# A decoder layer on one core: the feed-forwards' 22 tiles grouped 4, 10, 8 in place of 6, 8, 8

## The chip, the cores and the metric

The kernel runs on one core of a Trainium2 chip. The time is in device microseconds, from the start to the end of the program on that core; lower is better. TensorE (PE) multiplies matrices, VectorE (DVE) and ScalarE (ACT) work elementwise, GpSimd (POOL) does small side work, and SyncE (SP) issues most of the DMAs.

## What is computed

One layer for 512 prompt tokens and 32 sample tokens, D_MODEL = 1024: a half-step feed-forward, a mixing block of two attention kinds, a second half-step feed-forward, and a gated embedding. The change concerns the two feed-forwards, which the reference computes as follows.

```
D_FF = 2816

def swiglu(h, w_in, w_out):
    gu = h @ w_in
    g, u = jnp.split(gu, 2, axis=-1)
    return (jax.nn.silu(g) * u) @ w_out

x = x + 0.5 * rmsnorm(swiglu(rmsnorm(x, f1_pre), f1_in, f1_out), f1_post)
...
x = x + 0.5 * rmsnorm(swiglu(rmsnorm(x, f2_pre), f2_in, f2_out), f2_post)
```

## The kernel before

All activations stay on chip, features on partitions and the T = 544 tokens in two halves of 272. Each fp32 product is made from three fp32r matmuls: an operand is split into a high part (a copy by ACT, `w_hi`, `a_hi`, `h_hi`) and a low part (what remains, a subtraction by DVE, `w_lo`, `a_lo`, `h_lo`), and TensorE adds high x high, low x high and high x low (helper `dense`, L584).

**Feed-forward.** D_FF is 22 tiles of 128 rows. They are worked in three groups, `GROUPS`. For each group, an up stage makes the group's h tiles (silu(gate) x up), and a down stage multiplies them by the group's columns of the output weight and adds 8 output tiles into `y`. The h tiles of one group lie in `h_hi` and `h_lo`, which hold `G_MAX` tiles each.

- The first group (`f1_up0`, `f2_up0`) is made by plain products: per tile 8 blocks of input features x gate and up x 3 x 2 halves = 96 matmuls.
- The later groups (`up1`, `up2`) are made by `up_mixed` (L796), a scheme of seven products of blocks instead of eight. It splits tokens, input features and gate/up in two each. One tile is 7 products of 4 feature blocks x 3 matmuls = 84 matmuls. For it DVE adds blocks of weights (`mix_front`, L2015 to L2020), and needs seven activation blocks.
- These activation blocks are built while the first group runs: `block_values` (L2070), `block_difference` and `block_sum` (L2084 to L2097) on DVE, then for each of seven `block_high` on ACT (L1465) and `block_low` on DVE (L2077). Blocks 3 to 6 overwrite the plain input `a_hi`, `a_lo`; so blocks 3 to 5 wait for `a_gone`, which TensorE raises while it works on the group's last plain tile.
- A down stage has 8 products of (group size) x 6 matmuls. Its product reads the h tiles in order and waits for each one's low part (`h_tiles`).

**Queues.** Every engine has its instructions in a fixed order, written by hand. On DVE a tile of the first group is: two multiplies that take the sums out of PSUM (`out_of`, L1995, L1996), the product with silu (`product_of`, L2102), `h_lo` (L2001), and the split of the next weights (L1880). ACT has silu (L1423), `h_hi` (L1428) and the weights' high part (L1303). In the first down stage ACT also takes every product out of PSUM (L1510). `plain_end` is the end of the first group: around the last plain tile it holds block copies, the last tile's chain, and the split of the second down weight.

**Weights.** Two raw slots and two split slots are used in turn. SP's load of weight tile w waits until tile w - 2 is split; ACT's copy of a weight waits until the product before last has ended (`psum_full`).

In other places of the program, buffers of later use lie over those of earlier ones: `proj` (the projections of the mixing block) shares its memory, `hold_h`, with the h tiles, and the weights of the output projection are placed into free parts of it:

```
GROUPS = (6, 8, 8)
PLAIN = GROUPS[0]
hold_h = sb("hold_h", [P, 24 * T])
PLACED[W0["out"] + 2] = (h_flat[0][:, 4 * T:4 * T + SLOT], h_flat[1][:, 0:SLOT])
```

Of the kernel before, what the change touches and what calls it, by code (L numbers as in the profile page):

```python
# [18 lines left out]
ACT = mybir.ActivationFunctionType  # L19

P = 128
D_MODEL = 1024
SEQ = 512
DEC_BATCH = 8
# [14 lines left out]
GROUPS = (6, 8, 8)  # L39
G_FIRST = (0, 6, 14)  # L40
# [77 lines left out]
def build(nc, a, o):  # L118
# [13 lines left out]
    with ctx:  # L132
# [34 lines left out]
        kl_new = sb("kl_new", [N_SAMPLE, P])  # L167
# [7 lines left out]
        glr = sb("glr", [GLA_RANK, 2, HALF])  # L175
# [25 lines left out]
        hold_h = sb("hold_h", [P, 24 * T])  # L201
# [12 lines left out]

        work_flat = work[:].rearrange("p a t -> p (a t)")
# [153 lines left out]
        for name in (f"f1_down{ENDS}", f"f2_down{ENDS}"):  # L369
            for n in range(4):  # L370
                PLACED[W0[name] + 4 + n] = tuple(t_[:, G_MAX * P * n:G_MAX * P * (n + 1)] for t_ in a_flat)
# [923 lines left out]
        def _(act):  # L1295
# [171 lines left out]
            def plain_end(name):  # L1467


                f, up0, down0, st = int(name == "f2"), f"{name}_up0", f"{name}_down0", Step(PLAIN - 1)  # L1470
                split(st, up0, ticket(st, up0)[0])
                for n in range(3, 6):
                    act.wait_ge(sig["a_gone"], 3 * f + n - 2)
                    block_high(f, n)
                split(Step(0), down0, ticket(Step(0), down0)[0])
                up_gate(up0, st)
                up_high(up0, st)
                block_high(f, 6)
                act.wait_ge(sig["t_lo"], 7 * f + 4)
                down_first(Step(0), *ticket(Step(0), down0))  # L1480
# [92 lines left out]
            up("f1_up0")(Step(3), *ticket(Step(3), "f1_up0"))  # L1573
            stage("f1_up0", PLAIN, up("f1_up0"), first=4, end=PLAIN - 1)
# [30 lines left out]
            def keys_out(p):  # L1605
                act.wait_ge(sig["klt_full"], p + 1)
                if p:

                    act.wait_ge(sig["u_full"], p)
                    act.wait_ge(sig["klb_ready"], p)  # L1610
                fn(kl_nat, PS[:, 7, :].rearrange("p (c n) -> p c n", c=N_CH), ACT.Copy)
                fn(kl_new[:], PS[0:N_SAMPLE, 6, 64:64 + P], ACT.Copy).then_inc(sig["klt_out"], 1)
# [172 lines left out]
            split_edge("out", 1, T0["merge"])  # L1785
            split_edge("out", 2, T0["merge"])
# [24 lines left out]
            split_edge("f2_up0", 4, T0["f2_up0"] + 2)  # L1811
# [3 lines left out]
            up("f2_up0")(Step(3), *ticket(Step(3), "f2_up0"))  # L1815
            stage("f2_up0", PLAIN, up("f2_up0"), first=4, end=PLAIN - 1)
# [55 lines left out]
        def _(dve):  # L1872
# [231 lines left out]
            def plain_end(name, j):  # L2104
# [4 lines left out]
                split(st, up0)  # L2109
# [112 lines left out]
            up("f1_up0", 0)(Step(3), *ticket(Step(3), "f1_up0"))  # L2222
            stage("f1_up0", PLAIN, up("f1_up0", 0), first=4, end=PLAIN - 1)
# [24 lines left out]
            v.tensor_tensor(glr[:], PS[0:GLA_RANK, 4 * quad:4 * quad + 2, 0:HALF], rstd[0:GLA_RANK, 0],  # L2248
# [101 lines left out]
            def new_keys(p):  # L2350

                dve.wait_ge(sig["klt_out"], p + 1)
                if p:
                    dve.wait_ge(sig["sn_full"], 4 * p)
                v.tensor_tensor(kl_batch, kl_new[:].unsqueeze(1).broadcast_to([N_SAMPLE, DEC_BATCH, P]),
                                batch_mask[0:N_SAMPLE, :].unsqueeze(2).broadcast_to([N_SAMPLE, DEC_BATCH, P]),
                                ALU.mult).then_inc(sig["klb_ready"], 1)
# [260 lines left out]
            split_edge("f2_up0", 4)  # L2618
# [11 lines left out]
            up("f2_up0", 4)(Step(3), *ticket(Step(3), "f2_up0"))  # L2630
            stage("f2_up0", PLAIN, up("f2_up0", 4), first=4, end=PLAIN - 1)
# [313 lines left out]
```

## Time and profile before

| | |
|---|---|
| Median of 3 runs | 1181.22 us (1180.56 to 1181.26) |
| Span of the profiled execution | 1178.6 us |
| TensorE busy | 1159.9 us, 98%, 9234 matmuls |
| VectorE busy | 778.8 us, 66% |
| ScalarE busy | 548.2 us, 47% |
| First feed-forward, from the first matmul | 7.3 to about 374 us |
| Second feed-forward | about 739 to 1092 us |

A matmul's start-to-start distance is shorter than its duration, since they are pipelined: the mean of one is 290 ns, but 432 of them fill 54.31 us. "Idle before" in brackets is the time that an engine stood before an instruction, and what it then waited for. The chain of work that ended last tells which engine sets the end.

### The profile page before, as it was taken

How to read it: one execution, taken by the hardware profiler on the slowest of the kernel's cores; microseconds unless marked ns; L12 is line 12 of the kernel's file. 1: busy time of each engine (PE TensorE's matmuls, PEld its weight loads, DVE VectorE, ACT ScalarE, POOL GpSimd, SP SyncE). 2: the span in 40 equal slices, each digit the busy share in tenths (PEclk: the TensorE clock that was granted, in tenths of full speed). 3: DMA queues.
4: the chain of work that ended last, by engine and by line, in shares of the span. 5: the costliest groups of instructions: out<-in, count | busy, mean ns of one | idle time of the engine just before them, and what ended most of it. 6: DMA issues, size and time to landing. Idle time of an engine off the chain costs nothing.

```text
span 1178.6 us, 23067 instructions
## 1 busy us (share of the span) xinstructions
PE 1159.9 (98%) x9234; PEld 1120.3 (95%) x9234; DVE 778.8 (66%) x1076; ACT 548.2 (47%) x759; POOL 105.6 (9%) x138
## 2 busy tenths in 40 slices
PE   7999999999999999999999999999999999999997
PEld 7999999999999999999877699999999999999996
DVE  6853887368844965655379737863788458864766
ACT  5433555235543532312368745533555225543655
POOL 1600000000002012122050010000000000002102
PEclk9999999999999999999999999999999999999999
DMA  6213331232224032213047151113421233215202
GB/s 220 86 30 132 112 107 54 90 131 91 81 72 152 12 108 73 72 57 113 1 152 241 58 179 37 42 56 100 140 85 64 90 125 107 89 54 178 74 1 76
DMA packets 45404, 110.27 MB, mean 94 GB/s; under 512 B 5458, under 2 KB 11618, under 8 KB 45202
## 3 DMA queue, kind: packets, MB, share of 16 engines
q1 hardware_dynamic: 43522, 103.13, 26.2%
q0 software_dynamic: 1232, 5.01, 1.2%
q8 instruction: 54, 0.88, 0.3%
q10 hardware_dynamic: 576, 1.08, 0.2%
q14 instruction: 20, 0.16, 0.1%
HBM read 103.57 MB, written 5.64 MB: 93 GB/s over the span
## 4 chain that ended last, share of the span: by engine, by line
PE 91%; DVE 5%; ACT 3%; issue 1%; DMA 1%; ACTq 0%; DVEq 0%
PE PS L584 42%; PE PS L796 29%; PE PS L597 11%; PE PS L916 1%; PE PS L766 1%; PE PS L620 1%; PE PS L943 1%; DMA raw<-in_f_in 1%; PE PS L976 1%; ACT w_hi L1303 0%; PE PS L979 0%; DVE w_extra L2453 0%; PE PS L1020 0%; DVE extra L2440 0%; DVE w_lo L1880 0%
## 5 line engine op out<-in xcount | busy, mean ns | idle before, releaser
L1303 ACT ACTIVATE w_hi<-raw 128x1024 fp32r<-128x1024 f32 (+2 forms) x77 | 93.2, 1210 | 154.4 <-PE PS L584 129.6
L1880 DVE TENSOR_TENSOR w_lo<-raw,w_hi 128x1024 fp32r<-128x1024 f32 (+2 forms) x76 | 107.9, 1420 | 83.1 <-ACT w_hi L1303 82.7
L796 PE MATMUL PS<-a_lo,w_hi 128*128 128x272 f32 x512 | 148.7, 290 | 0.0
L796 PE MATMUL PS<-a_hi,w_lo 128*128 128x272 f32 x512 | 147.6, 288 | 0.0
L584 PE MATMUL PS<-a_hi,w_hi 128*128 128x272 f32 x656 | 139.5, 294 | 8.1 <-DVE w_lo L2181 7.3
L796 PE MATMUL PS<-a_hi,w_hi 128*128 128x272 f32 x512 | 147.4, 288 | 0.0
L584 PE MATMUL PS<-a_lo,w_hi 128*128 128x272 f32 x656 | 136.4, 289 | 0.0
L584 PE MATMUL PS<-a_hi,w_lo 128*128 128x272 f32 x656 | 136.0, 289 | 0.0
L584 PE MATMUL PS<-h_hi,w_hi 128*128 128x272 f32 x576 | 119.5, 289 | 0.2
L584 PE MATMUL PS<-h_hi,w_lo 128*128 128x272 f32 x576 | 119.2, 288 | 0.0
L584 PE MATMUL PS<-h_lo,w_hi 128*128 128x272 f32 x576 | 118.8, 288 | 0.0
L584 PEld LDWEIGHTS PS<-a_hi,w_hi 128*128 128x128 f32 x656 | 103.2, 189 | 12.3 <-issue 10.4
L584 PEld LDWEIGHTS PS<-a_lo,w_hi 128*128 128x128 f32 x656 | 103.8, 190 | 0.0
L584 PEld LDWEIGHTS PS<-a_hi,w_lo 128*128 128x128 f32 x656 | 103.5, 190 | 0.0
L796 PE MATMUL PS<-b_tail,w_hi 128*128 128x272 f32 x512 | 98.0, 289 | 0.0
L796 PEld LDWEIGHTS PS<-a_hi,w_hi 128*128 128x128 f32 x512 | 96.6, 189 | 0.0
L796 PEld LDWEIGHTS PS<-a_hi,w_lo 128*128 128x128 f32 x512 | 96.4, 188 | 0.0
L796 PEld LDWEIGHTS PS<-a_lo,w_hi 128*128 128x128 f32 x512 | 96.1, 188 | 0.0
L584 PEld LDWEIGHTS PS<-h_hi,w_hi 128*128 128x128 f32 x576 | 90.5, 188 | 0.8 <-DVE h_lo L2001 0.6
L584 PEld LDWEIGHTS PS<-h_lo,w_hi 128*128 128x128 f32 x576 | 90.5, 189 | 0.0
L584 PEld LDWEIGHTS PS<-h_hi,w_lo 128*128 128x128 f32 x576 | 89.9, 189 | 0.0
L796 PEld LDWEIGHTS PS<-b_tail,w_hi 128*128 128x128 f32 x512 | 80.3, 188 | 0.0
(473 smaller groups left out, 2618.9 us busy)
## 6 DMA issues: line engine op xcount, KB each, us to landing
raw<-in_f_in SPq DMA_DIRECT2D x86, 512.0 KB, 4.0
raw<-in_f_out SPq DMA_DIRECT2D x64, 256.0 KB, 2.8
raw<-in_w_rest SPq DMA_DIRECT2D x40, 256.0 KB, 2.8
raw<-in_f_out SPq DMA_DIRECT2D x32, 192.0 KB, 2.4
raw<-in_w_out SPq DMA_DIRECT2D x8, 512.0 KB, 4.6
raw<-in_ple_w_gate SPq DMA_DIRECT2D x8, 512.0 KB, 4.2
x<-in_x SPq DMA_DIRECT2D x8, 272.0 KB, 7.1
raw<-in_w_in SPq DMA_DIRECT2D x4, 512.0 KB, 4.1
```

The lines of the kernel that those rows point to most:

```text
L584: last = mm(PS[0:width, 4 * quad + 2 * c + half, 0:HALF], wt[:, cols], act[:, k, half * HALF:(half + 1) * HALF], start=(k == 0 and n == 0) ...
L597: last = mm(PS[0:width, 4 * quad + 2 * c + half, 0:HALF], wt[:, cols], act[:, k, tok], start=(k == 0 and n == 0), stop=(k == n_k - 1 and n ...
L620: last = mm(PS[:, 4 * quad + 2 + half, 0:HALF], ones[:], squares[:, tok], start=(k < summed), stop=(k == KD - 1))
L766: last = mm(PS[:, 4 * (t % 2) + 2 * c + half, 0:HALF], wt[:, slot, col:col + P], act[:, k, half * HALF:(half + 1) * HALF], start=(k == 0 a ...
L796: last = mm(PS[:, 4 * quad + bank, 0:HALF], w_[:, k * P:(k + 1) * P], a_[:, k, :], start=(start and k == 0 and i == 0), stop=(stop and k = ...
L916: last = mm(PS[:, 2 + hh, tok], k_[r, tok], q_[r, tok], start=True, stop=True)
L943: last = mm(PS[:, 7, n * 256:n * 256 + 256], kl_batch[:, 2 * part + n, :], gv_new[:, p * 256:(p + 1) * 256], start=True, stop=True)
L976: last = mm(PS[:, 2 + hh, tok], gv_nat[:, c, h * P:(h + 1) * P], att[p][:, N_CH * hh + c, :], start=True, stop=(c == 0))
L1303: fn(pair[0][:, 0:width], raw[:, slot, 0:width], ACT.Copy).then_inc(sig["split_hi"], 1)
L1880: v.tensor_tensor(pair[1][:, 0:width], raw[:, slot, 0:width], pair[0][:, 0:width].bitcast(F32), ALU.subtract).then_inc(sig["split_lo"], 1)
```

## The change

`GROUPS` becomes (4, 10, 8): the first group of each feed-forward has 4 plain tiles, the second 10 mixed tiles, the third 8 as before. So two tiles of each feed-forward pass from `dense` to `up_mixed`.

`h_hi` and `h_lo` grow to 10 tiles each. Memory for that comes from three places: `kl_new` gets a place in a buffer that holds `glr`, the GpSimd DMAs' descriptor scratch is halved to 8192 bytes, and `hold_h` is 28 instead of 24 rows of T. As the h buffers reach further into the projections, the third weight tile of the output projection now lies over keys of the mixing block, and ACT waits for the store of these keys (`k_stored`) before it writes there.

The steps of tiles 3 to 5 in the first group go: tile 3 is now the one that `plain_end` handles, and the split after tile 2 is already that of the first down weight.

```
-GROUPS = (6, 8, 8)
-G_FIRST = (0, 6, 14)
+GROUPS = (4, 10, 8)
+G_FIRST = (0, 4, 14)
...
-        kl_new = sb("kl_new", [N_SAMPLE, P])
...
-        glr = sb("glr", [GLA_RANK, 2, HALF])
+        glr_all = sb("glr_all", [P, 2, HALF])
+        glr = glr_all[0:GLA_RANK]
...
-        hold_h = sb("hold_h", [P, 24 * T])
+        hold_h = sb("hold_h", [P, 28 * T])
...
+        kl_new = scratch(glr_all[:].rearrange("p a t -> p (a t)"), 0, [N_SAMPLE, P])
...
-                split(st, up0, ticket(st, up0)[0])
...
-            up("f1_up0")(Step(3), *ticket(Step(3), "f1_up0"))
-            stage("f1_up0", PLAIN, up("f1_up0"), first=4, end=PLAIN - 1)
             plain_end("f1")
...
+            act.wait_ge(sig["k_stored"], 16)
             split_edge("out", 2, T0["merge"])
...
-            split_edge("f2_up0", 4, T0["f2_up0"] + 2)
+            split(Step(3), "f2_up0", ticket(Step(3), "f2_up0")[0])
...
-            up("f2_up0")(Step(3), *ticket(Step(3), "f2_up0"))
-            stage("f2_up0", PLAIN, up("f2_up0"), first=4, end=PLAIN - 1)
             plain_end("f2")
...
-                split(st, up0)
                 block_low(f, 3)
                 block_low(f, 4)
                 out_of(up0, j, st, t, quad, use)
...
-            up("f1_up0", 0)(Step(3), *ticket(Step(3), "f1_up0"))
-            stage("f1_up0", PLAIN, up("f1_up0", 0), first=4, end=PLAIN - 1)
             block_low(0, 2)
             plain_end("f1", 0)
...
-    nc = bacc.Bacc("TRN2", target_bir_lowering=False, num_devices=1)
+    nc = bacc.Bacc("TRN2", target_bir_lowering=False, num_devices=1, dynamic_dma_scratch_size=8192)
```

VectorE's queue of the kernel before, first feed-forward, from the low part of h tile 2 (L2001) to the last plain tile's chain. L1995 and L1996 take a tile out of PSUM, L2077 is `block_low`; the line numbers of the two kernels differ by three.

```order
L2001 TENSOR_TENSOR h_lo<-work,h_hi 128x544
L1880 TENSOR_TENSOR w_lo<-raw,w_hi 128x2048
L2097 SCALAR_TENSOR_TENSOR y<-extra,y 128x4x272
L1995 TENSOR_TENSOR work<-PS,rstd 128x544
L1996 TENSOR_TENSOR work<-PS,rstd 128x544
L2102 TENSOR_TENSOR work<-work 128x544
L2001 TENSOR_TENSOR h_lo<-work,h_hi 128x544
L1880 TENSOR_TENSOR w_lo<-raw,w_hi 128x2048
L1995 TENSOR_TENSOR work<-PS,rstd 128x544
L1996 TENSOR_TENSOR work<-PS,rstd 128x544
L2102 TENSOR_TENSOR work<-work 128x544
L2001 TENSOR_TENSOR h_lo<-work,h_hi 128x544
```

The same queue of the changed kernel, from the same instruction:

```order
L1998 TENSOR_TENSOR h_lo<-work,h_hi 128x544
L1877 TENSOR_TENSOR w_lo<-raw,w_hi 128x512
L2094 SCALAR_TENSOR_TENSOR y<-extra,y 128x4x272
L2074 TENSOR_TENSOR b_tail<-y,b_tail 128x1088
L2074 TENSOR_TENSOR a_lo<-y,a_hi 128x1088
L2074 TENSOR_TENSOR a_lo<-extra,a_hi 128x1088
L1992 TENSOR_TENSOR work<-PS,rstd 128x544
L1993 TENSOR_TENSOR work<-PS,rstd 128x544
L2099 TENSOR_TENSOR work<-work 128x544
L1877 TENSOR_TENSOR w_lo<-raw,w_hi 128x512
L1998 TENSOR_TENSOR h_lo<-work,h_hi 128x544
```

Between the sum L2097 (now L2094) and the next take-out stood nothing; now three `block_low` stand there, and that take-out belongs to the last plain tile.

ScalarE's queue at the same place, before. L1423 is silu, L1428 `h_hi`, L1465 `block_high`:

```order
L1428 ACTIVATE h_hi<-work 128x544
L1465 ACTIVATE b_tail<-y 128x1088
L1423 ACTIVATE work<-work 128x544
L1428 ACTIVATE h_hi<-work 128x544
L1303 ACTIVATE w_hi<-raw 128x2048
L1423 ACTIVATE work<-work 128x544
L1428 ACTIVATE h_hi<-work 128x544
L1303 ACTIVATE w_hi<-raw 128x768
L1465 ACTIVATE a_hi<-y 128x1088
L1465 ACTIVATE a_hi<-extra 128x1088
L1465 ACTIVATE a_hi<-hold_h 128x1088
L1303 ACTIVATE w_hi<-raw 128x768
```

and in the changed kernel, where these are L1424, L1429 and L1466:

```order
L1429 ACTIVATE h_hi<-work 128x544
L1466 ACTIVATE b_tail<-y 128x1088
L1466 ACTIVATE a_hi<-y 128x1088
L1466 ACTIVATE a_hi<-extra 128x1088
L1466 ACTIVATE a_hi<-hold_h 128x1088
L1304 ACTIVATE w_hi<-raw 128x512
L1424 ACTIVATE work<-work 128x544
L1429 ACTIVATE h_hi<-work 128x544
```

The four `block_high` stand in one row, behind `h_hi` of tile 2 and ahead of the second down weight's copy.

## Rows read from the trace of the kernel before

**Rows 1.** The page: busy time of engines; the chain that ended last.

```profile
PE 1159.9 (98%) x9234; PEld 1120.3 (95%) x9234; DVE 778.8 (66%) x1076; ACT 548.2 (47%) x759; POOL 105.6 (9%) x138
...
PE 91%; DVE 5%; ACT 3%; issue 1%; DMA 1%; ACTq 0%; DVEq 0%
```

**Rows 2.** The chain by time, two pieces: start us, us, what.

```profile
29.44 54.31 PE PS L584 x432
...
120.18 84.75 PE PS L796 x672
```

**Rows 3.** TensorE at down0's start: start us, us, instruction, idle before.

```profile
83.58 0.42 PE L584 MATMUL PS<-h_hi,w_hi 128*128 128x272 f32 x2
...
87.59 0.30 PEld L584 LDWEIGHTS PS<-h_hi,w_hi 128*128 128x128 f32 x2 [0.31 <-DVE h_lo L2001]
...
799.14 0.30 PEld L584 LDWEIGHTS PS<-h_hi,w_hi 128*128 128x128 f32 x2 [0.31 <-DVE h_lo L2001]
```

**Rows 4.** Timeline, ACT and DVE at down0's end; then load medians.

```profile
106.79 0.63 ACT L1510 ACTIVATE y<-PS 128x544 f32 x1 [3.16 <-PE PS L584]
...
108.18 0.96 DVE L1880 TENSOR_TENSOR w_lo<-raw,w_hi 128x768 fp32r<-128x768 f32 x1 [3.56 <-ACT w_hi L1303]
...
113.98 0.69 DVE L2015 TENSOR_TENSOR hold_w<-raw 128x512 f32<-128x512 f32 x1 [0.34 <-DMA raw<-in_f_in]
...
115.91 0.69 DVE L2020 TENSOR_TENSOR sq<-hold_w,raw 128x512 f32<-128x512 f32 x1
...
117.84 1.76 DVE L2023 TENSOR_TENSOR w_lo<-raw,w_hi 128x1536 fp32r<-128x1536 f32 x1 [1.24 <-ACT w_hi L1436]
...
819.73 0.96 DVE L1880 TENSOR_TENSOR w_lo<-raw,w_hi 128x768 fp32r<-128x768 f32 x1 [3.54 <-ACT w_hi L1303]
...
825.98 0.69 DVE L2015 TENSOR_TENSOR hold_w<-raw 128x512 f32<-128x512 f32 x1 [0.78 <-DMA raw<-in_f_in]
...
raw<-in_f_in SPq DMA_DIRECT2D x86, 512.0 KB, 4.0
```

**Rows 5.** Timeline of DVE and ACT, plain tiles of the first feed-forward.

```profile
53.96 2.28 DVE L1880 TENSOR_TENSOR w_lo<-raw,w_hi 128x2048 fp32r<-128x2048 f32 x1
...
56.16 1.28 DVE L2097 SCALAR_TENSOR_TENSOR y<-extra,y 128x1088 f32<-128x1088 f32 x1
...
57.48 1.12 ACT L1465 ACTIVATE b_tail<-y 128x1088 fp32r<-128x1088 f32 x1 [4.58 <-DVE y L2097]
...
59.67 0.73 DVE L1995 TENSOR_TENSOR work<-PS,rstd 128x544 f32<-128x544 f32 x1 [2.23 <-PE PS L584]
...
75.34 1.28 DVE L2077 TENSOR_TENSOR b_tail<-y,b_tail 128x1088 fp32r<-128x1088 f32 x1
...
83.78 0.72 DVE L1995 TENSOR_TENSOR work<-PS,rstd 128x544 f32<-128x544 f32 x1 [3.59 <-PE PS L584]
...
86.81 0.72 DVE L2001 TENSOR_TENSOR h_lo<-work,h_hi 128x544 fp32r<-128x544 f32 x1
```

**Rows 6.** Timeline of DVE and ACT, plain tiles of the second feed-forward.

```profile
762.01 2.29 DVE L1880 TENSOR_TENSOR w_lo<-raw,w_hi 128x2048 fp32r<-128x2048 f32 x1
...
772.37 1.29 DVE L2097 SCALAR_TENSOR_TENSOR y<-extra,y 128x1088 f32<-128x1088 f32 x1
...
773.69 1.11 ACT L1465 ACTIVATE b_tail<-y 128x1088 fp32r<-128x1088 f32 x1 [5.60 <-DVE y L2097]
```

**Rows 7.** TensorE's first matmuls; windows at the end: busy, PEclk.

```profile
7.30 0.79 PE L584 MATMUL PS<-a_hi,w_hi 128*128 128x272 f32 x2 [7.30 <-DVE w_lo L2181]
...
11.34 0.41 PE L584 MATMUL PS<-a_hi,w_hi 128*128 128x272 f32 x2
...
1172.00:1174.00 2.00, 0.17 (x1) 0.00 (x0) 1.96 (x5) 0.54 (x2) 0.00 (x0) 1.00 0.94 328
...
1175.00:1176.00 1.00, 0.00 (x0) 0.00 (x0) 0.00 (x0) 0.00 (x0) 0.00 (x0) 0.52 1.05 359
```

**Rows 8.** Timeline of GpSimd: the store of the keys.

```profile
555.46 0.55 POOL L2833 DMA_DIRECT2D out<-proj  x1
```

More of the change, by code:

```diff
@@ L370, in build @@
             for n in range(4):
-                PLACED[W0[name] + 4 + n] = tuple(t_[:, G_MAX * P * n:G_MAX * P * (n + 1)] for t_ in a_flat)
+                PLACED[W0[name] + 4 + n] = tuple(t_[:, GROUPS[ENDS] * P * n:GROUPS[ENDS] * P * (n + 1)] for t_ in a_flat)
         tail_flat = b_tail[:].rearrange("p a b k t -> p (a b k t)")
@@ L1611, in keys_out @@
                 fn(kl_nat, PS[:, 7, :].rearrange("p (c n) -> p c n", c=N_CH), ACT.Copy)
-                fn(kl_new[:], PS[0:N_SAMPLE, 6, 64:64 + P], ACT.Copy).then_inc(sig["klt_out"], 1)
+                fn(kl_new, PS[0:N_SAMPLE, 6, 64:64 + P], ACT.Copy).then_inc(sig["klt_out"], 1)
             act.wait_ge(sig["small_in"], 32)
@@ L2247, in _ @@
             full(dve, t)
-            v.tensor_tensor(glr[:], PS[0:GLA_RANK, 4 * quad:4 * quad + 2, 0:HALF], rstd[0:GLA_RANK, 0],
+            v.tensor_tensor(glr, PS[0:GLA_RANK, 4 * quad:4 * quad + 2, 0:HALF], rstd[0:GLA_RANK, 0],
                             ALU.mult).then_inc(psum_free[quad], 1)
@@ L2354, in new_keys @@
                     dve.wait_ge(sig["sn_full"], 4 * p)
-                v.tensor_tensor(kl_batch, kl_new[:].unsqueeze(1).broadcast_to([N_SAMPLE, DEC_BATCH, P]),
+                v.tensor_tensor(kl_batch, kl_new.unsqueeze(1).broadcast_to([N_SAMPLE, DEC_BATCH, P]),
                                 batch_mask[0:N_SAMPLE, :].unsqueeze(2).broadcast_to([N_SAMPLE, DEC_BATCH, P]),
@@ L2617, in _ @@
             block_difference(1, 0)
-            split_edge("f2_up0", 4)
+            split(Step(3), "f2_up0")
             st = Step(2)
@@ L2629, in _ @@
             block_sum(1, 1)
-            up("f2_up0", 4)(Step(3), *ticket(Step(3), "f2_up0"))
-            stage("f2_up0", PLAIN, up("f2_up0", 4), first=4, end=PLAIN - 1)
             block_low(1, 2)
```

## Prediction

> **What bounds the kernel now.** Read the chain of work that ended last: TensorE holds 91% of it [rows 1]. The long pieces of that chain show how densely: 432 plain matmuls in 54.31 us without a break, and 672 matmuls of a mixed group in 84.75 us [rows 2]. So TensorE's number of matmuls sets the time of a feed-forward, as long as VectorE (DVE) and ScalarE (ACT) have the next operands ready. The places where they are only just ready matter more here than averages. There are two in each feed-forward. The first is the step from the plain tiles to the first down projection (down0): in both feed-forwards TensorE's weight load waits 0.31 us for the last h tile's low part [rows 3]. The second is the step from down0 to the first mixed group [rows 4]. Nothing waits there now, but I shall show how little room is left.
>
> **What the change takes away.** A plain tile is 96 matmuls, at 54.31 / 432 = 0.1257 us each 12.07 us. A mixed tile is 7 products of 4 x 3, so 84 matmuls, at 84.75 / 672 = 0.1261 us each 10.59 us [rows 2]. Two tiles of each feed-forward pass from plain to mixed: 4 x (12.07 - 10.59) = 5.9 us less. The down projections keep their matmuls (22 h tiles x 8 x 6 in all), only cut 4 + 10 + 8 instead of 6 + 8 + 8. So down0's product is 24 matmuls (3.02 us) instead of 36 (4.52 us), down1's is 60 instead of 48. The longer down1 has more cover than before, and its wider weight split (1280 columns) falls into 7.5 us of product; the mixed group of 10 is the same loop run more often. Both at nothing.
>
> **First cost: the step from plain tiles to down0.** Down0's product reads its h tiles in order and can run until it needs the last one. That is 5 tiles of 6 matmuls, 3.77 us of cover, before; now 3 tiles, 2.26 us. Before, the last tile's chain on DVE began at 83.78, ended with the low part at 86.81 + 0.72, and TensorE went on at 87.59 [rows 3, 5]: 3.81 us. The narrower weight split in this chain (512 columns for 768) takes some 0.06 us off, since the h tile's own ACT copy is next late: 3.75 us. With that alone the wait would grow by 1.4 us.
>
> But the order on DVE moves too. The copies of the blocks for the mixed products (L2077, 1.28 us each; DVE starts its next instruction 0.08 us before the end, as at 53.96 and 56.16, so one every 1.20 us [rows 5]) were spread over two more tiles. Now three of them stand between the sum L2097 and the last tile's chain. In the first feed-forward: the split before the sum takes 0.69 instead of 2.28 us (the 512-wide DVE row at 113.98 [rows 4]), so the sum starts at 56.16 - 1.59 = 54.57 and ends at 55.85. ACT's copy of that block follows its end by 0.04 and takes 1.12, to 57.01 [rows 5]. Then DVE copies three low parts, 57.04 + 3 x 1.20 = 60.64 (ACT's copies take 1.12 us and stay ahead), and only then takes up the last tile, 1.0 us later than the 59.67 at which tile 3 was taken up before [rows 5]. TensorE gets the last low part at 60.64 + 3.75 = 64.39. It begins down0 two plain tiles earlier, 83.58 - 24.14 = 59.44, and runs dry at 61.70 [rows 3]. **Wait 2.7 us in place of 0.25** (87.59 less 83.58 + 30 x 0.1257): cost 2.5 us.
>
> In the second feed-forward DVE is later by itself, as the blocks are made while the first tiles run. The split at 762.01 shrinks from 2.29 to 0.69, everything after moves up by 1.6 us, and the sum at 772.37 starts at 770.77, ends 772.06 [rows 6]. ACT's copy to 773.21, three low parts to 776.84, chain to 780.59. Down0 began at 799.14 - 0.25 - 3.77 = 795.12 before [rows 3], begins at 770.98 now and runs dry at 773.24. **Wait 7.35 us in place of 0.25**: cost 7.1 us. Bounds for both together: if the copies cost no queueing, 1.4 each (2.8); if a copy waits for ACT's one in each case, up to 1 us more each (11.6). I take 9.6, since the order of the queues is fixed and every duration has a row.
>
> **Second cost: the step from down0 to the mixed group.** Its weights are 1 MB. The load starts when down0's seventh weight tile is split, and that waits on the product two places back. Before: ACT takes out product 4 at 106.79, the split ends at 108.18 + 0.96 = 109.14, the first sum of the new weights starts at 113.98, four sums and the low part follow (113.98, 115.91, 117.84 + 1.76 = 119.60) [rows 4], and TensorE needs them at about 120.0. The low part waited for ACT's copy there; without that it starts 2.55 us after the first sum. After: both splits are narrower by about 0.2 and 0.27 us, so from taking out product 4 (call it 0) the split ends at 1.86, the load lands at 1.86 + 4.84 = 6.70, the low part ends at 6.70 + 2.55 + 1.76 = 11.01, TensorE starts at 11.06. It ran out at three products later, 3 x 3.02 - 0.28 = 8.78. **Wait 2.3 us**, where there was none. In the second feed-forward the load took 825.98 - 820.69 = 5.29 us (the split at 819.73 takes 0.96) [rows 4], so 2.75 us. Together 5.0. Bounds: 1.8 us more each if the next 1 MB load, which now starts 3.0 instead of 4.5 us after this one, shares its bandwidth; 1 us less each if the load lands as early as the 4.0 us median of its halves [rows 4]. I take 5.0, from the two pairs of rows.
>
> A page of the Trainium skill prices the load otherwise: "DMA: Bandwidth & Descriptors", section "Anatomy of one DMA", gives about 2.0 us plus the bytes at 436 GB/s for one GpSimd-issued transfer, an estimate of 4.4 us for 1 MB; the rows of this case say 4.84 and 5.29. By the page the waits would be 1.3 us shorter together.
>
> Down0's inner steps stay covered: the split ends 1.86 us after a product is taken out, the running product 3.02 - 0.28 = 2.74 after it, so 0.9 us are left on each of the six. If that room were gone, each tenth of a microsecond would cost 0.6 us in a feed-forward.
>
> **Third cost: TensorE's clock.** At the start TensorE stood for 7.3 us, and its first matmuls come 0.22 to 0.23 us apart, half speed, until 11.34 [rows 7]: 18 matmuls took 4.04 instead of 2.26 us, 1.8 us lost. At the end its last matmul is over by 1172.2, and from 1175 on the granted clock is 0.52, the 1.2 GHz level [rows 7]. So a rest of 2.8 us was followed by the lower level there. The new rest of 7.4 us lies far beyond, so I add 1.8 us once. The three shorter ones (2.7, 2.3, 2.75 us) lie just at or under that 2.8; I take nothing for them and keep 5.4 us as the bound.
>
> The Trainium skill, "TensorE: Matmul & The Clock Gate", section "HAM oscillation", says that waits between bursts of matmuls put the clock back down, so that each burst starts slow. [...]
>
> **At nothing:** ACT's new wait for the stored keys stands ahead of the out-projection splits near 665 us; the store is issued at 555.46 [rows 8], a hundred microseconds earlier. The halved scratch serves GpSimd's few DMAs, none of which anyone waits for. If it delayed one, 1 us on the key store would still be hidden. The two moved small buffers change no instruction.
>
> **The sum.** -5.9 + 2.5 + 7.1 + 2.3 + 2.75 + 1.8 = +10.5 us. The profiled execution spans 1178.6 us and the median is 1181.22, 2.6 us outside the span, which the change doesn't touch. Forecast 1191.8 us.
>
> **Rivals.**
> 1. The clock holds through the 7.4 us rest: 1190.0. For it, no rest within the run before shows a fall, all being short; against it, both ends of the run. 0.12.
> 2. The clock falls in shorter waits too: one of them 1193.6, all three 1197.2. The tail shows the fall after 2.8 us; against it, TensorE was thinly used before that tail and densely before these. 0.18.
> 3. Half the stalls: the load lands early and DVE's copies fit better, some 4 us less, 1185 to 1188. 0.08.
> 4. The other side: the saved matmuls stand and the cover suffices. This is one mechanism, the last plain tile's chain on DVE and the load behind it both finishing inside down0's shorter products; then -5.9, 1175.3. It decides where the four waits sum to under 5.9 us, 40% of what I get. For it: ACT and DVE are 47% and 66% busy only [rows 1], and down0's inner steps keep room. Against: the waits follow from queue order and one load, not from averages. 0.06 faster, and 0.03 that it comes out even.
>
> The likeliest case has 0.53. The range reaches over rivals 1, one extra clock fall, and most of 3: 1186.5 to 1196.5. A measurement of this kernel can tell about 0.2%, 2.4 us, from no change: faster by more 0.06, within 0.03, slower 0.91.
>
> **What the profile after would show.** TensorE's count falls by 48 to 9186. At about 62 us and 773 us TensorE waits for the h tile's low part, 2.7 and 7.4 us; at about 85 and 806 it waits for the mixed weights' low part, 2.3 and 2.8 us. Matmuls after the 7 us rest stand 0.23 us apart for some 18. If the waits at 62 and 773 are equal, my reading of DVE's order is wrong; if there are none before the mixed group, the load was issued or landed earlier than I hold.

## The result: 1.1% slower

| | before | after |
|---|---|---|
| Median | 1181.24 us (4 runs) | 1194.14 us (4 runs, 1191.35 to 1195.09) |
| Ratio to before | | 1.0108, 95% interval 1.0096 to 1.0121 |
| Span of the profiled execution | 1178.6 us | 1192.5 us |
| TensorE's matmuls | 9234 | 9186 |

The forecast was 1191.8 us, slower. The median lies 2.3 us above it, inside the range.

The page of the changed kernel, to be read against [rows 1]: busy time, the granted clock in the 40 slices, and the shares of the chain that ended last.

```profile
PE 1159.1 (97%) x9186; PEld 1119.1 (94%) x9186; DVE 795.1 (67%) x1100; ACT 560.6 (47%) x779; POOL 105.7 (9%) x138
...
PEclk9999999999999999999999999989999999999999
...
PE 84%; DVE 9%; ACT 3%; issue 2%; DMA 2%; SPq 0%; DVEq 0%; ACTq 0%
```

48 matmuls are gone, yet TensorE's busy time fell by 0.8 us only, mostly since some of the others ran at half speed (the 8 in the clock's row is the longest such stretch). In the chain TensorE's share went from 91% to 84% and DVE's from 5% to 9%: there are now stretches in which TensorE does not set the end. The list of TensorE's waits (what waited for, sum, times, longest) names them:

```profile
PE PS L585 <- DVE h_lo L1998: 9.6, 2, 7.1
PE PS L585 <- DVE w_lo L2177: 7.0, 1, 7.0
PE PS L797 <- DVE w_lo L2020: 5.7, 2, 2.9
```

The middle one is the start of the program and was there before. The other two are the two steps of the prediction, each once per feed-forward. The first step in the first feed-forward, VectorE and TensorE (start us, us, instruction, idle before):

```profile
57.02 1.29 DVE L2074 TENSOR_TENSOR b_tail<-y,b_tail 128x1088 fp32r<-128x1088 f32 x1 [1.18 <-ACT b_tail L1466]
...
60.63 0.72 DVE L1992 TENSOR_TENSOR work<-PS,rstd 128x544 f32<-128x544 f32 x1
...
63.59 0.72 DVE L1998 TENSOR_TENSOR h_lo<-work,h_hi 128x544 fp32r<-128x544 f32 x1
...
61.47 0.41 PE L585 MATMUL PS<-h_hi,w_lo 128*128 128x272 f32 x2
64.37 0.52 PE L585 MATMUL PS<-h_hi,w_hi 128*128 128x272 f32 x2 [2.50 <-DVE h_lo L1998]
```

Three block copies run from 57.02 to 60.63, only then is the last tile taken out, and TensorE, dry since 61.72 (61.47 and two matmuls), goes on at 64.37: 2.65 us. In the second feed-forward the same rows stand later against TensorE, because the sum L2094 is later:

```profile
774.73 1.29 DVE L2094 SCALAR_TENSOR_TENSOR y<-extra,y 128x1088 f32<-128x1088 f32 x1
...
780.81 0.72 DVE L1992 TENSOR_TENSOR work<-PS,rstd 128x544 f32<-128x544 f32 x1
...
777.00 0.41 PE L585 MATMUL PS<-h_hi,w_lo 128*128 128x272 f32 x2
784.55 0.82 PE L585 MATMUL PS<-h_hi,w_hi 128*128 128x272 f32 x2 [7.15 <-DVE h_lo L1998]
```

Dry from 777.25 to 784.55, 7.3 us. The second step, down0 to the mixed group, answers to [rows 4]: the last split before the load (L1877), the first use of the loaded weights (L2012), their low part (L2020), and TensorE at both of its ends.

```profile
78.80 0.69 DVE L1877 TENSOR_TENSOR w_lo<-raw,w_hi 128x512 fp32r<-128x512 f32 x1 [2.38 <-ACT w_hi L1304]
...
84.93 0.69 DVE L2012 TENSOR_TENSOR hold_w<-raw 128x512 f32<-128x512 f32 x1 [2.49 <-DMA raw<-in_f_in]
...
87.47 1.75 DVE L2020 TENSOR_TENSOR w_lo<-raw,w_hi 128x1536 fp32r<-128x1536 f32 x1
...
86.03 0.41 PE L585 MATMUL PS<-h_hi,w_lo 128*128 128x272 f32 x2
89.27 0.52 PE L797 MATMUL PS<-b_extra,w_hi 128*128 128x272 f32 x2 [2.84 <-DVE w_lo L2020]
...
812.07 0.52 PE L797 MATMUL PS<-b_extra,w_hi 128*128 128x272 f32 x2 [2.90 <-DVE w_lo L2020]
```

The split ends at 79.49, the weights are used from 84.93: 5.44 us (5.57 in the second feed-forward, from 802.15 to 807.72). TensorE stands for 3.0 us here, and for 3.06 there.

Last the clock, in windows: busy time with counts for each engine, granted clock, DMA share, GB/s.

```profile
90.00:93.00 3.00, 3.00 (x18) 3.00 (x17) 2.97 (x5) 0.40 (x1) 0.00 (x0) 0.59 0.81 268
...
785.00:790.00 5.00, 5.00 (x24) 5.00 (x24) 2.59 (x3) 1.14 (x2) 0.00 (x0) 0.50 0.24 72
812.00:815.00 3.00, 2.93 (x23) 2.93 (x24) 2.97 (x5) 0.62 (x2) 0.00 (x0) 1.00 0.55 137
```

After the 7.3 us rest TensorE ran at its 1.2 GHz level until 790.16: 24 matmuls in 5.61 us instead of 3.02, so 2.6 us lost. After the 3.0 us wait of the first feed-forward the clock fell too, but late: the matmuls are 0.125 us apart from 89.27 to 90.51 and 0.22 apart behind it. The mixed group there took 107.71 us for its 840 matmuls, the same group in the second feed-forward, behind a wait of 3.06 us, took 106.20 at full clock: 1.5 us.

The account of the span: -5.9 (matmuls) + 2.4 (2.65 for 0.25) + 7.05 (7.3 for 0.25) + 3.0 + 3.06 + 2.6 + 1.5 = 13.7 us. Measured: 1192.5 - 1178.6 = 13.9. The medians are 12.9 apart, since the profiled execution of the changed kernel (1194.62 us) was 0.5 us above its median, and 2.1 us of it lay outside the span where I had counted 2.6.

### The profile page after: what moved, and what is told of

Same layout as the page of the kernel before. It is cut to its first block, busy times and chain, and to the rows that moved or that the text cites. A ratio compares the mean times of both kernels' runs of the same rounds, so it can differ in the third digit from the quotient of the medians.

```text
span 1192.5 us, 23120 instructions
## 1 busy us (share of the span) xinstructions
PE 1159.1 (97%) x9186; PEld 1119.1 (94%) x9186; DVE 795.1 (67%) x1100; ACT 560.6 (47%) x779; POOL 105.7 (9%) x138
## 4 chain that ended last, share of the span: by engine, by line
PE 84%; DVE 9%; ACT 3%; issue 2%; DMA 2%; SPq 0%; DVEq 0%; ACTq 0%
PE PS L585 33%; PE PS L797 32%; PE PS L598 10%; DMA raw<-in_f_in 2%; PE PS L917 1%; PE PS L767 1%; PE PS L621 1%; PE PS L944 1%; DVE w_lo L1877 1%; PE PS L977 0%; DVE work L2099 0%; DVE hold_h L2067 0%; ACT w_hi L1304 0%; PE PS L980 0%; DVE h_lo L1998 0%
## 5 line engine op out<-in xcount | busy, mean ns | idle before, releaser
L797 PE MATMUL PS<-a_lo,w_hi 128*128 128x272 f32 x576 | 166.5, 289 | 0.0
L797 PE MATMUL PS<-a_hi,w_lo 128*128 128x272 f32 x576 | 166.4, 289 | 0.0
L1304 ACT ACTIVATE w_hi<-raw 128x1024 fp32r<-128x1024 f32 (+3 forms) x73 | 85.6, 1172 | 168.0 <-PE PS L585 138.9
L1877 DVE TENSOR_TENSOR w_lo<-raw,w_hi 128x1024 fp32r<-128x1024 f32 (+3 forms) x72 | 98.8, 1373 | 73.2 <-ACT w_hi L1304 73.2
L797 PE MATMUL PS<-b_tail,w_hi 128*128 128x272 f32 x576 | 111.4, 291 | 0.0
L585 PE MATMUL PS<-a_lo,w_hi 128*128 128x272 f32 x528 | 110.0, 290 | 0.0
L585 PE MATMUL PS<-a_hi,w_lo 128*128 128x272 f32 x528 | 109.8, 289 | 0.0
L797 PEld LDWEIGHTS PS<-a_hi,w_hi 128*128 128x128 f32 x576 | 108.5, 188 | 0.0
L797 PEld LDWEIGHTS PS<-a_hi,w_lo 128*128 128x128 f32 x576 | 108.4, 188 | 0.0
L797 PEld LDWEIGHTS PS<-a_lo,w_hi 128*128 128x128 f32 x576 | 108.3, 188 | 0.0
L585 PEld LDWEIGHTS PS<-h_hi,w_hi 128*128 128x128 f32 x576 | 91.6, 190 | 10.3 <-DVE h_lo L1998 10.1
L585 PEld LDWEIGHTS PS<-a_hi,w_hi 128*128 128x128 f32 x528 | 83.4, 190 | 11.8 <-issue 10.2
L797 PEld LDWEIGHTS PS<-b_tail,w_hi 128*128 128x128 f32 x576 | 91.5, 190 | 0.0
L1437 ACT ACTIVATE w_hi<-raw 128x1536 fp32r<-128x1536 f32 x36 | 53.7, 1491 | 69.4 <-PE PS L797 55.4
L585 PEld LDWEIGHTS PS<-a_lo,w_hi 128*128 128x128 f32 x528 | 83.9, 191 | 0.0
```

Of the source, the lines that this page charges most:

```text
L585: last = mm(PS[0:width, 4 * quad + 2 * c + half, 0:HALF], wt[:, cols], act[:, k, half * HALF:(half + 1) * HALF], start=(k == 0 and n == 0) ...
L797: last = mm(PS[:, 4 * quad + bank, 0:HALF], w_[:, k * P:(k + 1) * P], a_[:, k, :], start=(start and k == 0 and i == 0), stop=(stop and k = ...
L1304: fn(pair[0][:, 0:width], raw[:, slot, 0:width], ACT.Copy).then_inc(sig["split_hi"], 1)
L1437: fn(w_cols(name[:2], 0, 3)[0], raw[:, slot, 0:3 * BLOCK], ACT.Copy).then_inc(sig["split_hi"], 1)
L1877: v.tensor_tensor(pair[1][:, 0:width], raw[:, slot, 0:width], pair[0][:, 0:width].bitcast(F32), ALU.subtract).then_inc(sig["split_lo"], 1)
```

## The experiments

Every kernel was run beside the kernel before on the same chip. On the first chip that had medians of 1180.67 and 1180.79 us (21 runs each), on the second of 1180.53 us (13 runs).

**1. The memory part alone**, groups 6, 8, 8 as before.

```
 GROUPS = (6, 8, 8)
...
-        hold_h = sb("hold_h", [P, 24 * T])
+        hold_h = sb("hold_h", [P, 28 * T])
...
+            act.wait_ge(sig["k_stored"], 16)
...
+ ..., dynamic_dma_scratch_size=8192)
```

> The kernel before, groups 6, 8, 8, with the change's memory part alone: the DMAs' scratch halved, kl_new in the glr buffer, hold_h of 28 rows, ScalarE's wait for the key store. Theory (the time comes from waits of TensorE that the new grouping makes): within 0.5 us of before, 1181.2. Rival (the halved scratch or the new wait costs something): 1183 or more, with the wait seen near 665 us.

1180.68 us, ratio 0.9999 (0.9990 to 1.0008). The halved scratch, the moved buffers and the wait for the keys cost nothing that can be measured; all 12.9 us are the grouping's.

**2. The last tile's chain ahead of the block copies.** The changed kernel; DVE and ACT take up the last plain tile first and make blocks 2 to 6 behind it, while down0 runs.

```
-                block_low(f, 3)
-                block_low(f, 4)
                 out_of(up0, j, st, t, quad, use)
                 product_of(up0, st, quad, use)
                 split(Step(0), f"{name}_down0")
                 up_low(up0, st)
-                block_low(f, 5)
-                block_low(f, 6)
+                block_low(f, 2)
+                block_low(f, 3)
+                split(Step(1), f"{name}_down0")
+                for c in range(2, 5):
+                    split(Step(c), f"{name}_down0")
+                    block_low(f, c + 2)
...
```

ScalarE's queue is turned in the same way.

> The changed kernel with one order turned: on ScalarE and VectorE the last plain tile's chain stands ahead of the block copies, which follow during down0. Theory (the queue order makes 1.0 us of the first and 4.9 us of the second wait): TensorE's wait at down0 falls from 2.65 to about 1.7 us and from 7.3 to about 2.4 us, and the slow clock after the long one goes (2.5 us): about 8 us less than the changed kernel, 1185 to 1187. Rival (VectorE has simply too much work in that stretch, the order doesn't matter): the copies are then late for a later step, a new wait comes up, and the time stays at 1192 to 1195.

1186.99 us (1185.15 to 1188.57), ratio 1.0059. The waits for the last h tile fell from 9.6 to 3.8 us, and the other step's stayed:

```profile
PE PS L797 <- DVE w_lo L2025: 5.4, 2, 3.0
PE PS L585 <- DVE h_lo L2003: 3.8, 2, 2.3
```

The medians are 7.2 us apart, at the edge of what I expected. The profiled execution was the fastest of the five (1185.15 us), and its span is 9.5 us shorter than the changed kernel's: 5.8 us of that is the first step's waiting, 0.3 the second's, 0.8 the start of the program, which differs between executions of one kernel too (down0 began 0.8 us sooner here), and 2.6 the clock. That fell once (behind the 3.0 us wait that had ended at 801.07; low from 802.4 to 805.8 us, 1.5 us lost) where it had cost 4.1. Its mean is 0.998 there for 0.993, and 0.995 to 0.996 in the other four. So the place of the block copies in the two queues is shown to be the cause of most of the first step's wait. Of what stays, 1.5 us in each is the chain against the shorter cover; the other 0.8 us in the second feed-forward is the block sum (L2094, L2099 in this kernel), which still stands ahead of the take-out: VectorE takes the tile out at 772.29, while ScalarE could begin its copy at 771.54.

**3. The first mixed tile's weights early.** The changed kernel; their 1 MB goes into h tiles that are still free, before the load of down0's fifth weight tile.

```
+        mix_raw = hold_h[:, 4 * T:4 * T + SLOT]
...
+                    if n == 0:
+                        for c in range(4):
+                            load(w0 + c, ...)
+                        for c in range(2):
+                            sp.dma_start(mix_raw[:, c * 1024:(c + 1) * 1024], src[:, c * 1024:(c + 1) * 1024]) ...
```

> The changed kernel with the first mixed tile's 1 MB weight loaded early, into h tiles that are free in the first group, in place of behind down0's seventh weight. Theory (the wait of 3.0 us before each mixed group is the load's landing): the sums on VectorE start at once, TensorE's wait falls to about 1.3 us in each feed-forward, and no clock fall follows it: 3.3 us less, 5 where the clock fell: 1188.5 to 1190.5. Rival (VectorE's and ScalarE's own steps set that wait): unchanged, 1192 to 1195.

1190.35 us (1189.08 to 1191.65), ratio 1.0083: 3.8 us less than the changed kernel.

```profile
PE PS L611 <- DVE h_lo L2024: 9.6, 2, 7.1
...
PE PS L823 <- DVE w_lo L2046: 2.0, 2, 1.0
```

The other step is untouched and this one is down to 1.0 us each. So what was late there was the load; the 1.0 us left is ACT's and DVE's high and low part of 1536 columns. The clock fell behind the first feed-forward's wait of about 2.6 us (low from 64.9 to 68.4 us), and behind the long rest it was low from 778.3 to 785.2 us, so that only 12 matmuls behind the restart at 782.26 were slow and 1.4 us were lost.

**4. Both edits.**

> Both of the two edits above on the changed kernel. Theory: the gains add: waits of about 1.7, 2.4, 1.3 and 1.3 us, no clock fall, 1193.7 - 5.9 - 2.5 - 3.3 - about 1 = 1181 to 1183, level with before. Rival (the two waits hide one another or the mixed tiles cost more than their 84 matmuls): 1185 or more.

1181.52 us (1180.39 to 1183.05, 11 runs), ratio 1.0004 (0.9995 to 1.0013). The waits are those that each edit had left (3.8 and 1.8 us). The two edits together give back 12.6 us, alone 7.2 and 3.8; the 1.6 us beyond that sum are within the scatter of the changed kernel. The clock fell once even here, behind the wait of 2.3 us in the second feed-forward (low from 775.4 to 778.8 us), which cost 1.5 us. Counted from where TensorE ran dry, as in the account of the span above, the four waits are 6.2 us. So the account is -5.9 (matmuls) + 6.2 - 0.5 (the two waits that were there before) + 1.5 (clock) - 0.8 (down0 began at 58.68 us; the kernel before's 83.58 less two plain tiles is 59.44) = +0.5 us, and the span is 0.7 us longer than before.

**5. A rest in the kernel before.** To price a rest apart from the regrouping, DVE makes the low part of block 4 five or nine more times in the second feed-forward, one behind the other and ahead of the last plain tile.

```
+                if f:
+                    for i in range(5):
+                        v.tensor_tensor(B_PAIR[4][1], B_RAW[4], B_PAIR[4][0].bitcast(F32), ALU.subtract) ...
```

> The kernel BEFORE, with nothing changed but a delay: on VectorE in feed-forward 2, ahead of the last plain tile's chain, the low copy of block 4 is made five more times (about 1.3 us each, 6.5 in all, of which 3.8 lies under down0's five covered h tiles), so that TensorE rests about 2.5 to 3 us at the plain to down0 step once. If a rest of this length costs its own length only: 1183.3 to 1183.9. If the granted clock falls behind it as it did once in the changed kernel behind a wait of 3.0 us: 1.8 to 2.5 us more, 1185.2 to 1186.2. My theory says that it can do either, so I expect a scatter between the two over the rounds, with a median of 1184 to 1185.

> The kernel BEFORE with the same delay made longer (nine more copies): TensorE rests about 7.5 to 8 us at feed-forward 2's plain to down0 step, once. My theory (a rest this long always lowers the granted clock for some 25 matmuls behind it, which costs 2.5 to 2.8 us): 1190.7 to 1191.7, and the records show the granted clock at its lower level behind the rest. Rival, a rest costs its own length only: 1188.2 to 1188.9.

1185.35 us (1184.25 to 1187.10) and 1191.10 us (1190.31 to 1191.45). The profile of the first shows TensorE's rest and the clock behind it:

```profile
801.89 0.82 PE L584 MATMUL PS<-h_hi,w_hi 128*128 128x272 f32 x2 [3.04 <-DVE h_lo L2001]
...
802.00:804.00 2.00, 2.00 (x9) 2.00 (x10) 2.00 (x2) 0.32 (x2) 0.00 (x0) 0.50 0.61 197
```

The second:

```profile
807.41 0.82 PE L584 MATMUL PS<-h_hi,w_hi 128*128 128x272 f32 x2 [8.35 <-DVE h_lo L2001]
...
809.00:811.00 2.00, 2.00 (x11) 2.00 (x11) 1.15 (x2) 1.35 (x2) 0.00 (x0) 0.50 0.15 57
```

A rest of 3.04 us made the median 4.6 us longer: 12 matmuls at half speed (801.89 to 804.78) lost 1.4 us beside it. One of 8.35 us made it 10.3 us longer: 18 matmuls (807.41 to 811.66) lost 2.0. Counted from where TensorE ran dry, the rests are 3.2 and 8.5 us. Less the 0.25 that was there before and with the clock that makes 4.35 and 10.25 us, so little is missing. The first median missed the 1184 to 1185 us that I expected: it lies where I had put a fall of the clock, not half-way to no fall. The second is in the expected range, but not by the expected terms: the rest came out 0.4 to 0.9 us longer than I put, and the clock's loss as much smaller. The rival without a loss of clock (1188.2 to 1188.9) falls.

**6. More cover.** As 4, and TensorE takes h tiles 0 to 2 for down0's first two products before it needs h tile 3. DVE also splits the first down weight ahead of the product with silu, not behind it.

```
+                for c in range(2):
+                    ...
+                    for k in range(PLAIN - 1):
+                        ...
+                            dense_half(quad, placed(down0, st), 1, k, PLAIN, H, half)
+                h_tiles(first)(PLAIN - 1)
+                for quad, pair in both:
+                    for half in range(2):
+                        last = dense_half(quad, pair, 1, PLAIN - 1, PLAIN, H, half)
```

> The kernel with both edits (the last plain tile's chain ahead of the block copies; the first mixed tile's weight loaded early: 1181.52 us, TensorE still waits 3.8 us in two waits for h_lo and 1.8 in two for w_lo), and now TensorE takes h tiles 0 to 2 of down0's first TWO products before it needs h tile 3, so that its cover is 6 h-tile pieces (4.5 us) and not 3 (2.26 us). My theory (the waits at plain to down0 are a chain of fixed length against a cover counted in products, and nothing else waits at that place): the wait of feed-forward 1 (1.5) goes to about 0, that of feed-forward 2 (2.3) to about 0.1, so the h_lo waits fall from 3.8 to under 0.5 us and the time to 1178.0 to 1178.8. Rival: the second down weight, now needed 2.3 us sooner, takes the wait over (its split stands behind the same copies): the waits keep their sum or nearly, and the time stays at 1181 to 1182. Rival 2: half of it, with 0.7 to 1.2 us left at feed-forward 2: 1179 to 1180.

1180.64 us (11 runs), 0.9 us less than 4 where I expected about 3. The waits for h tile 3 are gone as expected, and the first rival's wait for a down weight's low part is 0.5 us, once. But another wait, at the third product, took their place, 1.5 us in each feed-forward, so that the first feed-forward gained nothing. Its rows in the first, TensorE, DVE and ACT:

```profile
65.04 0.29 PE L624 MATMUL PS<-h_hi,w_lo 128*128 128x272 f32 x1
66.83 0.51 PE L611 MATMUL PS<-h_hi,w_hi 128*128 128x272 f32 x2 [1.50 <-ACT y L1560]
...
64.81 1.28 DVE L2122 TENSOR_TENSOR a_lo<-y,a_hi 128x1088 fp32r<-128x1088 f32 x1
...
66.12 1.14 ACT L1560 ACTIVATE y<-PS 128x544 f32<-128x544 f32 x2 [0.87 <-DVE a_lo L2122]
```

ACT writes down0's first result over `y`, from which DVE still reads blocks 2 and 3. The copies that experiment 2 moved out of the way are late here: until ACT has emptied the first buffer in PSUM, TensorE cannot begin the third product. Neither of my rivals had named this one.

**7. The first 512 columns apart.** As 6, and the first mixed tile's high and low parts are made in two pieces, so that TensorE can begin with the first.

```
+                if cut:
+                    v.tensor_tensor(lo[:, 0:cut], mix_source(name, st, slot)[:, 0:cut], hi[:, 0:cut].bitcast(F32), ...)
...
+                    if early(name, st):
+                        pe.wait_ge(sig["first_lo"], 3 + (f == "f2"))
```

> As the run before (two products of down0 together), and the first mixed tile's high and low parts of the weight are made with their first 512 columns apart, so that TensorE can begin the mixed group's first block when those stand, not when all 1536 columns do. The wait for w_lo in the kernel with the early load is 0.9 us at each feed-forward (1.8 in all), and the copy of the low part takes 1.75 us for 1536 columns, so about 0.6 for 512. My theory (what is left there is the length of the low copy behind the high one): both waits go to about 0, the time 1.5 to 1.8 us under the run before it, 1176.5 to 1177.0. Rival: the chunk costs an instruction and a wait of its own and the wait moves to the second block: no more than 0.5 us gained.

1178.57 us (1177.79 to 1179.15, 11 runs), ratio 0.9978 (0.9969 to 0.9987). Both waits before the mixed group went, 2.1 us less than 6. The time is above the range that I wrote because its base, 6, was; the gain over 6 is a little more than the 1.5 to 1.8 us expected. This version beats both kernels, the one before by 2.2 us, 0.2%.

**8. The blocks read from `y` ahead again**, in the first feed-forward alone, where both engines stand idle before the chain.

```
+                if not f:
+                    block_low(f, 2)
+                    block_low(f, 3)
                 out_of(up0, j, st, t, quad, use)
...
```

> The kernel with all edits so far (1178.57 us) still waits 1.50 us in each feed-forward at down0's third product: ScalarE may write down0's first result over y only when blocks 2 and 3, which are read from y, have their low parts, and VectorE makes these behind the last plain tile's chain (they end at 66.02, the copy of y starts at 66.06, TensorE resumes at 66.77). In feed-forward 1 both engines stand idle before that chain (VectorE from 55.39 to 59.21, ScalarE from 52.44 to 59.21). Here blocks 2 and 3 of feed-forward 1 alone go back ahead of the chain, the others stay behind it. My theory (the wait is for y's last reader): feed-forward 1's 1.50 goes and feed-forward 2's stays: 1176.8 to 1177.4. Rival (the wait is for the PSUM buffer, which only the copy's own length frees, 0.57 to 0.7 us after product 1's end, and the readers of y are no part of it): a wait of 0.6 to 1.2 stays in feed-forward 1, 1177.6 to 1178.3. Rival 2, the two blocks push the chain back by up to 1 us and the wait moves to h tile 3: 1178 to 1179.

1178.02 us (1177.08 to 1179.54, 9 runs), ratio 0.9978 (0.9968 to 0.9988): no measurable gain over 7, and above the 1176.8 to 1177.4 us of my theory. The reading of the wait was right, since that one is gone in the first feed-forward and stays in the second (1.5 us), but the next stood close behind it:

```profile
65.38 0.63 ACT L1352 ACTIVATE w_hi<-raw 128x512 fp32r<-128x512 f32 x1 [2.06 <-PE PS L624]
...
66.05 0.69 DVE L1940 TENSOR_TENSOR w_lo<-raw,w_hi 128x512 fp32r<-128x512 f32 x1 [1.96 <-ACT w_hi L1352]
...
66.88 0.51 PE L611 MATMUL PS<-h_hi,w_hi 128*128 128x272 f32 x2 [0.78 <-DVE w_lo L1940]
```

Both split slots are held by the two products that now run together, so the third weight tile can't be split before the first product ends, and TensorE waits 0.78 us for it. The time lies in the ranges of both rivals, but neither mechanism is what the rows show.

**9. The second mixed load held back** until the first has landed, and **the changed kernel again** as its pair.

```
+                        if n == 1:
+                            load(w1, slot, up(name, g0)(Step(0), slot))
+                            sp.wait_ge(raw_in[slot], 32 * (Step(0).half(w1) + slot))
```

> The changed kernel, and SyncE does not issue the second mixed tile's 1 MB load before the first tile's has landed (in the trace of the changed kernel it is issued at 82.6 us, with the first, from 79.67, under way until 84.9). Theory (the two loads share the DMA engines, so that the first takes 5.44 and 5.57 us, where I had put 4.84 and 5.29): the first load lands 0.3 to 0.6 us sooner, the two waits of 3.0 us become 2.5 to 2.7, and the time is 0.5 to 1.2 us under the changed kernel run beside it. Rival: the first half of the load is what the row shows and the second load takes nothing from it (it starts when the first is nearly done): waits and time as the changed kernel's, within 0.3 us.

> The changed kernel again, unchanged, as the pair of the run before and to see its scatter: 1194 us in the median. Theory (its scatter, 1191.35 to 1195.09 over four runs, comes from the clock, which falls behind the 7.3 us wait each time and behind each of the two 3.0 us waits and the 2.65 us wait in some executions): the runs lie between 1190.5 and 1196 in clusters about 1 to 2 us apart, while the kernel before stays within 1 us of its median but for single runs. Rival (the scatter is the DMAs'): the profiled execution shows load times that differ by as much as the spans, with the granted clock at its higher level behind all of the short waits.

1194.04 us (1191.03 to 1195.43, 4 runs) and 1196.07 us (1192.97 to 1199.17, 5 runs). The medians say nothing, as the two scatter by 4 and 6 us; the rows do. Those of the held kernel's split ahead of the load and of the load's first use:

```profile
79.94 0.69 DVE L1882 TENSOR_TENSOR w_lo<-raw,w_hi 128x512 fp32r<-128x512 f32 x1 [2.39 <-ACT w_hi L1309]
...
85.49 0.69 DVE L2017 TENSOR_TENSOR hold_w<-raw 128x512 f32<-128x512 f32 x1 [1.93 <-DMA raw<-in_f_in]
```

The changed kernel in this execution:

```profile
80.91 0.69 DVE L1877 TENSOR_TENSOR w_lo<-raw,w_hi 128x512 fp32r<-128x512 f32 x1 [2.39 <-ACT w_hi L1304]
...
86.50 0.69 DVE L2012 TENSOR_TENSOR hold_w<-raw 128x512 f32<-128x512 f32 x1 [1.97 <-DMA raw<-in_f_in]
```

The load took 4.86 us held back and 4.90 us not; in the second feed-forward 5.23 and 5.29. So the overlap with the next load took nothing here, and my theory on it falls: the same kernel's load took 5.44 and 5.57 in one execution and 4.90 and 5.29 in another. Had I set the held kernel against the first execution alone, its 4.86 us would have looked like a proof. The other traces say the same. Measured in this way, the load took 4.82 to 5.52 us in the first feed-forward and 5.26 to 5.78 in the second in four executions with groups 6, 8, 8 (before, and experiments 1 and 5), where the next load starts later; and 4.90 to 5.44 and 5.29 to 5.74 in three with 4, 10, 8 (the changed kernel twice, and experiment 2). What sets it within these ranges isn't shown.

The clock in the windows behind three of the changed kernel's four waits, and behind the fourth:

```profile
65.00:67.00 2.00, 1.82 (x8) 1.82 (x9) 2.00 (x3) 0.38 (x2) 0.00 (x0) 0.50 0.44 131
...
92.00:95.00 3.00, 3.00 (x15) 3.00 (x15) 2.97 (x4) 0.40 (x1) 0.00 (x0) 0.50 0.93 320
786.00:790.00 4.00, 3.85 (x17) 3.85 (x18) 3.19 (x4) 1.48 (x3) 0.00 (x0) 0.50 0.24 69
...
813.00:817.00 4.00, 3.68 (x29) 3.68 (x30) 3.97 (x6) 0.88 (x2) 0.00 (x0) 1.00 0.59 168
```

It fell three times in this execution and twice in the first, with the same waits but for 0.5 us. The fall behind the 2.65 us wait, absent in the first execution, cost 12 matmuls 2.88 instead of 1.51 us (65.18 to 68.06), 1.4 us. So the rival, by which the clock stays high behind all the short waits, falls. This execution had also begun down0 0.8 us later than the first (60.26 for 59.46). The kernel before, which has no such waits, stays within 1180.21 to 1181.83 over its 13 runs beside these, and between 1180.06 and 1182.87 in the 42 on the first chip.

But my expectation was missed as well: the median is 2 us above the 1194 that I wrote, and three of five runs lie above 1196. The longest, 1199.17 us, has the same mean clock (0.991) as one of 1195.71, so the clock as measured doesn't explain that difference, and as only one run was profiled it stays open. That the runs fall in clusters can't be told from nine of them.

## Why the prediction was right, and what was mis-sized

**Matmuls saved, -5.9.** Right. The count fell by 48. Experiment 7 has hardly a wait left but for the two at the third product, 1.66 us each from where TensorE ran dry: 1178.6 - 5.9 + 2 x 1.66 + 0.5 (a down weight) - 0.5 (the two waits of 0.25 that the kernel before had) = 1176.0 us of span, measured 1175.9.

**Plain tiles to down0, 2.7 and 7.35.** Right, 2.65 and 7.3. In the first feed-forward the order of DVE's queue and the durations of [rows 5] put every start of the chain within 0.1 us: 60.64 against 60.63, and TensorE's restart at 64.39 against 64.37. In the second every start came 4.0 us later than I wrote (TensorE's restart at 784.55, not 780.59), because I hadn't carried over what the first feed-forward loses; the distances between them hold. Experiment 2 shows the cause by taking the copies out of the way. One thing was read too simply. The listing of DVE's queue before the change ends with the chain of tile 4; the last plain tile there is tile 5, and three block copies stand between the two as well (75.34 to 80.19 us). They cost nothing only because DVE then stood idle for 3.59 us until TensorE had finished tile 5 [rows 5]. What the change took away is this slack, more than it changed the order.

**Down0 to the mixed group, 2.3 and 2.75.** The mechanism is right (experiment 3), the size was off in the profiled execution: 3.0 and 3.06. The term that failed is the load, put at 4.84 and 5.29 from one execution, measured 5.44 and 5.57. The second execution of the changed kernel has 4.90 and 5.29, and there the waits are about 2.5 and 2.8. The bound that I named for it, bandwidth shared with the next load, is not the reason (experiment 9). One pair of rows is one draw: with groups 6, 8, 8 this load took between 4.8 and 5.8 us, too. The estimate of 4.4 us by the Trainium skill's "DMA: Bandwidth & Descriptors", section "Anatomy of one DMA", whose fit is for GpSimd-issued transfers, is below every one of the 16 loads measured here (4.82 to 5.78 us).

**Clock, +1.8 once.** That the clock would fall behind the long rest was right; this term was mis-sized. The fall cost 2.6 us, not 1.8: I had taken the length of the slow stretch from the start of the program, as if it were fixed. The level fell while TensorE still stood, at 780.0 us, and rose at 790.3, and the 24 matmuls in the part behind the restart were slow. Behind an equal rest in experiment 3 there were 12 (1.4 us). And I took nothing for the three waits of 2.65 to 3.06 us, where rival 2 had one of them or all pay. One of three paid in the first execution, two in the second. The tail from which I had read that a rest of 2.8 us was needed was one draw, too: counted from where TensorE ran dry, the traces have 15 waits of 2.4 to 3.2 us, and the clock fell behind 9 of them, the shortest 2.42 us, the longest without a fall 3.06 us. Behind no wait of up to 1.7 us did it fall, and behind each of the five rests of over 7 us it did.

In the first execution the clock cost 4.1 us in place of 1.8; with the 1.0 us of the loads that makes 3.3 us over the forecast sum of 10.5, where 3.4 were measured. The likeliest case (1191.8) and rival 2 with one more fall (1193.6) were nearly the same case, and the measured median lies next to the latter: the range held because it was drawn over both.

The Trainium skill's section "HAM oscillation" in "TensorE: Matmul & The Clock Gate" tells of a kernel that waits about 3 to 5 us between bursts of matmuls and starts each burst slow. The rests of 7.3 us here agree with it each time, the waits near 3 us only sometimes, and some waits shorter than that kernel's paid as well.

**Down0's inner steps and the memory part, nothing.** Right: no wait stands there in the list, and experiment 1 shows the memory part alone.

**Rival 4** (the saved matmuls stand and the cover suffices) needed both the chain and the load to finish inside shorter products. Experiments 2, 3, 6 and 7 brought that about by hand, piece by piece, and reached 1178.0 to 1178.6 us, not the 1175.3 of the saved matmuls alone: each wait that was removed uncovered a shorter one behind it.

## What to carry to other kernels

When a group is made smaller, its product is the cover of everything that prepares the next stage: list what must be ready at its end (here a chain, three copies of another purpose in the same queue, and a 1 MB load) and set each against the shorter product, since the saved work is paid once and each uncovered chain is paid per stage. Copies with a late deadline belong behind a chain with an early one, but look for what overwrites their source, which is the next deadline. A wait of 2.4 to 3.2 us of a busy TensorE cost some 1.5 us more through the clock in 9 of 15 places, in one execution and not in the next, so such waits widen a kernel's scatter too. And a row that a forecast rests on (a load, a fall of the clock) is one draw, so look at the same row in a second execution before explaining a difference of half a microsecond.

## What the runs showed of the hardware

- The clock can fall after TensorE has resumed. Behind a wait of 3.0 us that had ended at 89.27 us the matmuls kept full speed until 90.51, and only then were 0.22 us apart, until about 93.9. Of the nine falls behind waits of 2.4 to 3.2 us, six came 0.8 to 1.3 us after the restart and three up to 0.5 us before it.
- How many matmuls are slow behind a long rest depends on when in the rest the clock fell: it was low for equally long in the changed kernel (780.0 to 790.3 us) and in the kernel with the 8.35 us rest (801.4 to 811.7), but 24 matmuls came behind the first restart (784.55) and 18 behind the second (807.41). Behind an equal 7.3 us rest in experiment 3 it was low for a shorter time (778.3 to 785.2) and 12 were slow. The cost of a fall was 1.4 to 2.6 us.
- Equal waits give unequal clocks: 3.0 us fell and 3.06 us did not in one execution; 2.65 us fell in one and not in the other; 2.42 us fell in experiment 4 and 2.43 us did not in experiment 2.
- The same 1 MB load of the same kernel took 4.90 and 5.44 us in two executions, from the end of the split that frees its buffer to its first use.
